# Attention in two layers: a pair's scores in three parts and its weighing in three rounds, each placed behind a round of turned blocks

## The chip, the cores and the metric

The kernel runs on one core of one Trainium2 chip, as one program. The metric is the device time of that core in microseconds, as the median of several runs. The profiled execution is one run with the hardware profiler.

The engines are named as in the profile: PE is TensorE (matmuls; PEld its weight loads), DVE is VectorE, ACT is ScalarE, POOL is GpSimd, SP the queue that issues DMAs.

## The reference, cut to what matters

The network has a first block of two layers (attention, then a mixture of experts) and a second block (gated linear attention, dilated attention, a feed-forward part). Only the attention of the first block's two layers is touched. There are 512 latent tokens and 256 context tokens, heads are 64 wide, everything is float32.

```python
def diff_attend(qb, k, v, lam):            # layer 0, four differential pairs
    s = jnp.einsum('bqhcd,bkhcd->bhcqk', qb, k).astype(jnp.float32) * ATTN_SCALE
    p = jax.nn.softmax(s, -1)
    a = p[:, :, 0] - lam * p[:, :, 1]
    return jnp.einsum('bhqk,bkhe->bqhe', a.astype(v.dtype), v)

def gqa_attend(qb, k, v):                  # layer 0, eight heads
    s = jnp.einsum('bqhgd,bkhd->bhgqk', qb, k).astype(jnp.float32) * ATTN_SCALE
    p = jax.nn.softmax(s, -1)
    return jnp.einsum('bhgqk,bkhd->bqhgd', p.astype(v.dtype), v)
```

Layer 1 has the same shape with a sink logit and a band of 128 positions (window attention) in eight heads, and a bias table over all latent keys (neighbourhood attention) in the other eight. Its queries are the 512 latents alone; layer 0 has the 256 context tokens as queries too, and these see the 256 context keys only.

## The kernel before, in words

`attention_phase` (L747 on) is called once for each layer. Its unit of work is a pair of heads for one tile of 128 queries, numbered u: eight pairs for each tile, `U` = 48 pairs in layer 0 (four latent tiles, two context tiles) and 32 in layer 1. `where(u)` gives tile n and pair p. In layer 0 the pairs p = 0 to 3 are differential (`diff` = 4): both heads' probabilities are combined into one matrix. The others, and all pairs of layer 1, keep two matrices. In layer 1 the order within a tile is: four neighbourhood pairs first, then four banded ones.

What a pair goes through:

- `score(u)` (TensorE, L943): S = q k for both heads, into `pS[u % 2]`, 1536 float32 wide, three PSUM banks. Head 0 has its operands on partitions 0-63, head 1 on 64-127. For 768 keys head 0 fills columns 0-767 and head 1 columns 768-1535, so the middle bank is shared by both (`second(u)` = 768). `pieces` cuts each head's columns at the banks; `joint` are the pieces in the shared bank, `alone` those in the outer banks. Joint pieces of head 0 come first, then the outer banks of both heads in turns, then the joint pieces of head 1. A matmul appears as two instructions in the profile. Where no more than 512 keys are seen (context queries: 256; banded pairs of the first and last tile: 512) the second head starts at column 1024 and nothing is shared. Banded pairs of the two middle tiles see 640 keys.
- `shift(u)` (VectorE): the row maximum. In layer 0 one reduction (L1145; two for 256-wide scores, L1147 and L1148) and a scaling (L1149); in layer 1 it also adds the mask or the bias and writes E (L1158, or L1163 and L1168, twice each). It waits for both `scored0` and `scored1`.
- `exp(u)` (ScalarE, L1073 or L1069): E = exp(...), two activations with row sums.
- `divide(u)` (VectorE): reciprocals (L1179); for pairs with two matrices also the scaling of head 0's (L1185). POOL scales the other head's (L929). For differential pairs `subtract(u)` (VectorE, L1192) combines both after POOL.
- `turn(u, k)` (TensorE, L974): up to four 128x128 blocks of E turned into `pT`, one bank. A round waits (`moved`) until the round before has been copied out. A pair with two matrices of 768 has 12 blocks, three rounds; of 640, rounds of 4, 4 and 2; of 512, two rounds of 4; a differential pair has 6 blocks, rounds of 4 and 2. Context pairs have one round.
- `move(u, k)`: pT to `PT[x % 4]`, four buffers. Round 0 of a pair with two matrices and more than one round is copied by VectorE (L1202), all others by ScalarE (L1084). The copy waits (`weighed`) until the buffer's contents of four rounds ago were used.
- `weigh(u, k)` (TensorE, L987 differential, L989 otherwise): probabilities times values, accumulated over the rounds in `pO`.
- `take_o(u)` (ScalarE, L1090): pO to SBUF.
- On VectorE, once for each tile of layer 0 at p = 6, four sums of squares (L1238).

The order on each engine is the order in which its code is written, with waits on semaphores between engines. TensorE's loop at L1025 is, for each u: turning round 0 of u; all scores of u+3; turning round 1; all weighing of u-1; turning round 2. ScalarE's is: copy 0 of u, exp of u+2, copy 1, take_o of u-1, copy 2. VectorE's is: `subtract(u + 1)`, copy 0 of u, then `shift(u + 3)` and `divide(u + 2)` (the other way round if pair u+2 is differential). Before it writes `pS[u % 2]`, `score(u)` waits until pair u-2 has been read: in layer 0 by exp (`e_ready`), in layer 1 by shift (`shifted`).

POOL also prepares eight rows of 1024 (L913 to L919) in layer 0 from pair 16 on, one at every second pair (four in layer 1). SP issues loads at the stage's start and waits for the last weighing before it issues the first expert weights. After the loop the output projection, the layer norm and the routing logits follow in the same stage.

Of the kernel before, what the change touches and what calls it, by code (L numbers as in the profile page):

```python
# [746 lines left out]
def attention_phase(nc, g, l, srcs, qT, kT, V, logits, na_bias):  # L747
# [11 lines left out]
    def where(u):  # L759

        return u // 8, (u + 4) % 8 if last_l else u % 8
# [18 lines left out]
    def pieces(u, b):  # L780

        out = []
        for i, k in enumerate(key_blocks(u)):
            at = b * second(u) + i * P
            if out and out[-1][0] // 512 == at // 512 and out[-1][1] + out[-1][2] == k * P:
                out[-1][2] += P
            else:
                out.append([at, k * P, P])
        return out

    def turns(u):

        n, p = where(u)
        return [(i, 0) for i in range(len(key_blocks(u)))] if p < diff else [(i, b) for i in range(len(key_blocks(u))) for b in range(2)]

    def rounds(u):
        return (len(turns(u)) + 3) // 4
# [7 lines left out]
    def k_chunk(p):  # L805
        if l == 0:
            return p if p < 4 else 4 + (p - 4) // 2
        return p // 2 if p < 4 else 2 + p - 4
# [7 lines left out]
    with Phase(nc) as ph:  # L816
# [29 lines left out]
        shared, scored0, scored1, shifted, e_ready, divided, readyD, readyP = (  # L846
            ph.sem(n) for n in ("shared", "scored0", "scored1", "shifted", "e_ready", "divided", "readyD", "readyP"))
# [10 lines left out]
        def tile(t):  # L858
            return slice(t * P, (t + 1) * P)
# [69 lines left out]
                pool.tensor_scalar(e, e, st[:, u % 4, 6 + b:7 + b], None, ALU.mult).then_inc(readyP, 1)  # L929
        @block.tensor  # L930
        def _(pe):
            def score(u):

                if u >= U:
                    return
                n, p = where(u)
                if u >= 2:
                    pe.wait_ge(shifted if last_l else e_ready, u - 1)

                def product(b, piece):  # L940
                    at, k0, w = piece
                    rows = slice(b * HD, (b + 1) * HD)
                    return pe.matmul(pS[u % 2][:, at:at + w], qT[rows, p, tile(n)], kT[rows, k_chunk(p), k0:k0 + w], start=True, stop=True)  # L943

                first, then = pieces(u, 0), pieces(u, 1)
                joint = [x for x in first if x[0] // 512 == 1], [x for x in then if x[0] // 512 == 1]
                alone = [x for x in first if x[0] // 512 == 0], [x for x in then if x[0] // 512 == 2]
                for x in joint[0]:
                    last = product(0, x)
                if joint[0]:  # L950
                    last.then_inc(shared, 1)
                for i in range(max(len(alone[0]), len(alone[1]))):
                    if i < len(alone[0]):
                        last0 = product(0, alone[0][i])
                    if i < len(alone[1]):
                        last1 = product(1, alone[1][i])
                last0.then_inc(scored0, 1)
                if joint[1]:
                    pe.wait_ge(shared, sum(second(v) == 768 for v in range(u + 1)))
                    for x in joint[1]:  # L960
                        last1 = product(1, x)
                last1.then_inc(scored1, 1)

            def turn(u, k):
                if k >= rounds(u):
                    return
                x = round_no(u, k)
                if k == 0:
                    pe.wait_ge(readyD, u + 1)
                    pe.wait_ge(readyP, u + 1)  # L970
                if x:
                    pe.wait_ge(moved, x)
                for j, (i, b) in enumerate(turns(u)[4 * k:4 * k + 4]):
                    last = pe.transpose(pT[:, tile(j)], E[:, u % NB, b, tile(i)], ident[:])  # L974
                last.then_inc(turned, 1)

            def weigh(u, k):
                if k >= rounds(u):
                    return
                (n, p), x, blocks = where(u), round_no(u, k), key_blocks(u)  # L980
                pe.wait_ge(moved, x + 1)
                if k == 0 and u:
                    pe.wait_ge(o_out, u)
                for j, (i, b) in enumerate(turns(u)[4 * k:4 * k + 4]):
                    c0, first, end = v_at(p, b), i == 0, i == len(blocks) - 1
                    if p < diff:
                        last = pe.matmul(pO[:, 0:P], PT[:, x % 4, j], V[:, blocks[i], c0:c0 + P], start=first, stop=end)  # L987
                    else:
                        last = pe.matmul(pO[b * HD:(b + 1) * HD, 0:P], V[:, blocks[i], c0:c0 + HD], PT[:, x % 4, j], start=first, stop=end)  # L989
                last.then_inc(weighed, 1)  # L990

            def turn_o(n):
                if n >= total:
                    return
                pe.wait_ge(o_ready, n + 1)
                if n:
                    pe.wait_ge(d_moved, n)
                for c in range(4):
                    last = pe.transpose(pT[:, tile(c)], o[:, n, tile(c)], ident[:])
                last.then_inc(d_turned, 1)  # L1000

            def mix(n, half, ks):
                for k in ks:
                    last = pe.matmul(pS[n % 2][:, half * 512:(half + 1) * 512], oT[:, k, tile(n)], wout[:, k, half * 512:(half + 1) * 512],  # L1004
                                     start=(k == 4), stop=(k == 3))
                return last

            def turn_f(n):
                pe.wait_ge(f_ready, n + 1)
                if n:  # L1010
                    pe.wait_ge(f_moved, 2 * n)
                for half in range(2):
                    for c in range(4):
                        last = pe.transpose(pS[half][:, 1024 + c * P:1024 + (c + 1) * P], f[:, half * 4 + c::C], ident[:])
                    last.then_inc(f_turned, 1)

            def route(n):
                pe.wait_ge(f_moved, 2 * n + 2)
                for k in range(C):
                    last = pe.matmul(pO[:, 36 * n:36 * n + 36], fT[:, k, :], wr[:, k, :], start=(k == 0), stop=(k == C - 1))  # L1020
                last.then_inc(routed, 1)

            for u in range(3):
                score(u)
            for u in range(U):  # L1025
                turn(u, 0)
                score(u + 3)
                turn(u, 1)
                if u:
                    for k in range(3):  # L1030
                        weigh(u - 1, k)
                turn(u, 2)
            for k in range(3):
                weigh(U - 1, k)
            pe.wait_ge(const_in, 16 * n_const)
            pe.wait_ge(o_out, U)
            pe.wait_ge(moved, round_no(U, 0))
            pe.wait_ge(shifted if last_l else e_ready, U)
            for n in range(total):
                if n >= 2:  # L1040
                    pe.wait_ge(x_used, n - 1)
                for half in range(2):
                    mix(n, half, range(4, 8))
                if diff:
                    if n == 0:
                        turn_o(0)
                    pe.wait_ge(d_moved, n + 1)
                    turn_o(n + 1)
                mix(n, 0, range(4))
                if n:  # L1050
                    turn_f(n - 1)
                mix(n, 1, range(4)).then_inc(mixed, 1)
                if n:
                    route(n - 1)
            turn_f(total - 1)
            route(total - 1)

        @block.scalar
        def _(act):
# [17 lines left out]
            def move(u, k):  # L1077
                if k >= rounds(u) or moved_by_vector(u, k):
                    return
                x, w = round_no(u, k), P * len(turns(u)[4 * k:4 * k + 4])  # L1080
                act.wait_ge(turned, x + 1)
                if x >= 4:
                    act.wait_ge(weighed, x - 3)
                act.activation(PT[:, x % 4].rearrange("p j n -> p (j n)")[:, 0:w], pT[:, 0:w], ACT.Copy).then_inc(moved, 1)  # L1084
# [13 lines left out]
            for u in range(U):  # L1098
                move(u, 0)
                exp(u + 2)  # L1100
                move(u, 1)
                if u:
                    take_o(u - 1)
                move(u, 2)
            take_o(U - 1)
            if diff:
                act.wait_ge(ss_ready, total)
# [1892 lines left out]
```

## Time and profile before

| what | us |
|---|---|
| median of 3 runs | 3447.9 (3446.75 to 3449.11) |
| profiled execution | 3446.33 |
| its span | 3444.5 |
| granted TensorE clock, mean | 0.942 |
| PE busy in the span | 2907.5 (84%) |
| pair loop of layer 0 in the span | about 282 to 482 |
| pair loop of layer 1 in the span | about 1330 to 1500 |

An instruction's row gives its start, its time, the engine and the line; neighbouring instructions of one kind are merged with their count. The end of a matmul is modelled, so the time that a block of matmuls takes is best read from its start to the start of the next block on the same engine. In brackets stands the idle time of the engine before the instruction and who released it.

### The profile page before, as it was taken

To read this page: it belongs to the slowest core of one execution; us is meant where nothing else is said; L and a number is where in the kernel's file an instruction comes from. 1 tells how busy PE (TensorE), PEld (TensorE's weight loads), DVE (VectorE), ACT (ScalarE), POOL (GpSimd) and SP (SyncE) were. 2 spreads that over 40 slices of the span, in tenths; PEclk is the share of its full clock that TensorE was granted. 3 is DMA by queue.
4 is the path that set the end of the run, shared out by engine and by line. 5 is a ranking of instruction groups with operands and counts; after the bars stand their busy time and mean duration, and the time that the engine had idled before them with its cause. 6 is when DMAs were issued, how large, how long until landed. Compare 5 with 4: busy or idle time off the path is not lost. (4 is left out here: it accounts for less than half of the span.)

```text
span 3444.5 us, 50705 instructions
## 1 busy us (share of the span) xinstructions
PE 2907.5 (84%) x20913; PEld 1623.6 (47%) x20913; DVE 1047.9 (30%) x2201; ACT 756.7 (22%) x1483; POOL 512.3 (15%) x632
## 2 busy tenths in 40 slices
PE   7998888678776698895866663999999999999999
PEld 4555654355444345653543332444444554544444
DVE  3425856311111444754111113443211231211101
ACT  2224641111111323620111112311112220200000
POOL 0003630233323002511322220000000000000000
PEclk8999999799999899997988886999999999999999
DMA  7833022999997642026899996112222122322237
GB/s 296 312 135 115 1 92 93 398 426 426 426 425 304 220 113 96 1 110 256 367 423 423 424 423 239 58 50 82 73 73 73 49 74 83 82 86 80 98 119 259
DMA packets 188525, 679.10 MB, mean 197 GB/s; under 512 B 52766, under 2 KB 94222, under 8 KB 163782
## 3 DMA queue, kind: packets, MB, share of 16 engines
q1 hardware_dynamic: 176550, 655.66, 49.0%
q0 software_dynamic: 11808, 21.03, 1.6%
q8 instruction: 127, 2.08, 0.2%
q14 instruction: 40, 0.33, 0.0%
HBM read 653.89 MB, written 33.98 MB: 200 GB/s over the span
## 5 line engine op out<-in xcount | busy, mean ns | idle before, releaser
L1677 PE MATMUL pH<-w,room 128*32 128x256 f32 x5504 | 340.0, 401 | 77.5 <-DMA w<-in_moe_w 77.5
L2744 PE MATMUL banks<-hT,wf 128*128 128x512 f32 (+2 forms) x768 | 303.2, 557 | 3.3 <-ACT hT L2801 2.9
L1677 PEld LDWEIGHTS pH<-w,room 128*32 128x32 f32 x5504 | 217.7, 116 | 184.7 <-issue 110.9
L1713 DVE TENSOR_TENSOR hh<-hs,pH 128x128 f32<-128x128 f32 x118 | 33.9, 287 | 794.0 <-ACT hs L1696 794.0
L929 POOL TENSOR_SCALAR E<-E,st 128x768 f32<-128x768 f32 (+3 forms) x80 | 168.0, 2100 | 661.3 <-DVE st L1179 660.7
L1684 PE MATMUL pY<-w,hT 128*32 128x256 f32 x2752 | 166.3, 381 | 107.9 <-DVE hT L1715 103.5
L2744 PEld LDWEIGHTS banks<-hT,wf 128*128 128x128 f32 x768 | 140.8, 190 | 164.6 <-issue 154.9
L416 PE MATMUL pa<-aT,w 128*128 128x512 f32 x416 | 205.7, 599 | 1.3 <-DVE aT L680 1.3
L1677 PE MATMUL pH<-room 128*32 128x256 f32 x2048 | 136.1, 424 | 57.7 <-DMA room<-in_moe_w 34.8
L1684 PEld LDWEIGHTS pY<-w,hT 128*32 128x32 f32 x2752 | 96.4, 109 | 177.8 <-issue 134.3
L2490 PE MATMUL pa<-hT,ring 128*128 128x512 f32 x384 | 167.8, 592 | 0.0
L2395 PE MATMUL pa<-hT,ring 128*128 128x512 f32 x384 | 165.0, 592 | 1.3 <-PEq L91 1.3
L974 PE MATMUL pT<-ident,E 128*128 128x128 f32 x672 | 114.6, 290 | 54.8 <-ACT PT L1084 31.2
L2783 PE MATMUL banks<-ring,aT 128*128 128x512 f32 x352 | 151.2, 592 | 0.0
L2042 PE MATMUL pa<-hT,ring 128*128 128x512 f32 x320 | 142.8, 603 | 0.0
L1004 PE MATMUL pS<-wout,oT 128*128 128x512 f32 x320 | 141.4, 594 | 0.8 <-issue 0.8
L1699 ACT ACTIVATE y<-pY 128x256 f32<-128x256 f32 x118 | 45.2, 383 | 418.2 <-PE pY L1684 418.2
L1640 POOL DMA_INDIRECT y<-y,at_y x122 | 125.9, 1032 | 60.9 <-POOL at_y L1660 59.7
L1677 PEld LDWEIGHTS pH<-room 128*32 128x32 f32 x2048 | 82.0, 122 | 106.7 <-issue 58.4
L974 PEld LDWEIGHTS pT<-ident,E 128*128 128x128 f32 x672 | 72.6, 144 | 100.3 <-issue 47.9
L1696 ACT ACTIVATE hs<-pH 128x128 f32<-128x128 f32 x118 | 32.7, 277 | 390.6 <-PE pH L1677 390.6
L943 PE MATMUL pS<-room 64*128 64x256 f32 (+2 forms) x608 | 110.7, 482 | 8.4 <-ACT E L1073 4.9
(483 smaller groups left out, 3957.8 us busy)
## 6 DMA issues: line engine op xcount, KB each, us to landing
w<-in_moe_w SPq DMA_DIRECT2D x144, 2048.0 KB
room<-in_moe_w SPq DMA_DIRECT2D x48, 2048.0 KB
mw<-in_mod_w SPq DMA_DIRECT2D x24, 2048.0 KB, 16.6
ring<-in_w_ff_down SPq DMA_DIRECT2D x33, 1024.0 KB, 4.8
ring<-in_w_in SPq DMA_DIRECT2D x15, 2048.0 KB, 8.2
ring<-in_w_gate SPq DMA_DIRECT2D x6, 2048.0 KB, 8.7
wf<-in_w_ff_gate SPq DMA_DIRECT2D x11, 1024.0 KB, 5.6
wf<-in_w_ff_up SPq DMA_DIRECT2D x11, 1024.0 KB, 8.0
```

The lines of the kernel that those rows point to most:

```text
L416: last = pe.matmul(pa[n % 2][:, 0:512], w[:, i % SLOTS_W, k, tile(c)], aT[:, k, 0:512], start=(k == 0), stop=(k == C - 1))
L929: pool.tensor_scalar(e, e, st[:, u % 4, 6 + b:7 + b], None, ALU.mult).then_inc(readyP, 1)
L974: last = pe.transpose(pT[:, tile(j)], E[:, u % NB, b, tile(i)], ident[:])
L1004: last = pe.matmul(pS[n % 2][:, half * 512:(half + 1) * 512], oT[:, k, tile(n)], wout[:, k, half * 512:(half + 1) * 512], start=(k == 4), ...
L1640: pool.indirect_dma_start(out=y_rows, out_offset=bass.IndirectOffsetOnAxis(ap=at_y[:, b:b + 1], axis=0), in_=y[:, b], in_offset=None, boun ...
L1677: last = pe.matmul(pH[strip(s), 0:2 * P].rearrange("p (j n) -> p j n", j=2), xT[:, k, :], slot_of(g, "w13", b)[:, :, k, s * P:(s + 1) * P] ...
L1684: last = pe.matmul(pY[strip(s), 0:YW], hT[:, k, :], slot_of(g, "w2", b)[:, k, s * YW:(s + 1) * YW], start=(k == 0), stop=(k == HC - 1))
L2042: last = pe.matmul(pa[b][:], ring[:, j % RING, i, tile(c)], hT[:, i, :], start=(i == 0), stop=(i == C - 1))
L2395: last = pe.matmul(pa[b][:], ring[:, j % RING, i, at], hT[:, i, :], start=(i == 0), stop=(i == C - 1))
L2490: last = pe.matmul(pa[b][:], ring[:, j % RING, k, (c % 4) * P:(c % 4 + 1) * P], hT[:, k, :], start=(k == 0), stop=(k == C - 1))
L2744: last = pe.matmul(banks[f % 2][:, j * 512 + cols.start:j * 512 + cols.stop], wf[:, i % 2, j, k, (f % 2) * P:(f % 2 + 1) * P], hT[:, k, co ...
L2783: last = pe.matmul(banks[b][:, h * 512:(h + 1) * 512], aT[:, f, tile(t)], wd[:, m % SLOTS_D, f % 2, h * 512:(h + 1) * 512], start=(f == 0) ...
```

## The change

`score(u)` gets a second argument. Part 0 is head 0's joint pieces (and the wait for the PSUM buffer), part 1 the outer banks of both heads, part 2 head 1's joint pieces. A pair without a shared bank has its whole score in part 1. For each u TensorE's order becomes: turning 0, weighing 0 of u-1, part 1 of u+3, turning 1, weighing 1 of u-1, part 2 of u+3, turning 2, weighing 2 of u-1, part 0 of u+4. On ScalarE `take_o(u - 1)` moves behind copy 2. The first three pairs' scores are still issued in one piece each.

```diff
--- before.py
+++ after.py
@@ -929,12 +929,12 @@
                 pool.tensor_scalar(e, e, st[:, u % 4, 6 + b:7 + b], None, ALU.mult).then_inc(readyP, 1)
         @block.tensor
         def _(pe):
-            def score(u):
+            def score(u, part):
 
                 if u >= U:
                     return
                 n, p = where(u)
-                if u >= 2:
+                if u >= 2 and part == 0:
                     pe.wait_ge(shifted if last_l else e_ready, u - 1)
 
                 def product(b, piece):
@@ -945,21 +945,24 @@
                 first, then = pieces(u, 0), pieces(u, 1)
                 joint = [x for x in first if x[0] // 512 == 1], [x for x in then if x[0] // 512 == 1]
                 alone = [x for x in first if x[0] // 512 == 0], [x for x in then if x[0] // 512 == 2]
-                for x in joint[0]:
-                    last = product(0, x)
-                if joint[0]:
+                if part == 0 and joint[0]:
+                    for x in joint[0]:
+                        last = product(0, x)
                     last.then_inc(shared, 1)
-                for i in range(max(len(alone[0]), len(alone[1]))):
-                    if i < len(alone[0]):
-                        last0 = product(0, alone[0][i])
-                    if i < len(alone[1]):
-                        last1 = product(1, alone[1][i])
-                last0.then_inc(scored0, 1)
-                if joint[1]:
+                if part == 1:
+                    for i in range(max(len(alone[0]), len(alone[1]))):
+                        if i < len(alone[0]):
+                            last0 = product(0, alone[0][i])
+                        if i < len(alone[1]):
+                            last1 = product(1, alone[1][i])
+                    last0.then_inc(scored0, 1)
+                    if not joint[1]:
+                        last1.then_inc(scored1, 1)
+                if part == 2 and joint[1]:
                     pe.wait_ge(shared, sum(second(v) == 768 for v in range(u + 1)))
                     for x in joint[1]:
                         last1 = product(1, x)
-                last1.then_inc(scored1, 1)
+                    last1.then_inc(scored1, 1)
 
             def turn(u, k):
                 if k >= rounds(u):
@@ -975,7 +978,7 @@
                 last.then_inc(turned, 1)
 
             def weigh(u, k):
-                if k >= rounds(u):
+                if u < 0 or k >= rounds(u):
                     return
                 (n, p), x, blocks = where(u), round_no(u, k), key_blocks(u)
                 pe.wait_ge(moved, x + 1)
@@ -1021,15 +1024,20 @@
                 last.then_inc(routed, 1)
 
             for u in range(3):
-                score(u)
+                for part in range(3):
+                    score(u, part)
             for u in range(U):
                 turn(u, 0)
-                score(u + 3)
+                weigh(u - 1, 0)
+                if u == 0:
+                    score(3, 0)
+                score(u + 3, 1)
                 turn(u, 1)
-                if u:
-                    for k in range(3):
-                        weigh(u - 1, k)
+                weigh(u - 1, 1)
+                score(u + 3, 2)
                 turn(u, 2)
+                weigh(u - 1, 2)
+                score(u + 4, 0)
             for k in range(3):
                 weigh(U - 1, k)
             pe.wait_ge(const_in, 16 * n_const)
@@ -1099,9 +1107,9 @@
                 move(u, 0)
                 exp(u + 2)
                 move(u, 1)
+                move(u, 2)
                 if u:
                     take_o(u - 1)
-                move(u, 2)
             take_o(U - 1)
             if diff:
                 act.wait_ge(ss_ready, total)
```

## Rows read from the trace of the kernel before

**Rows 1.** Table of stretches: busy time of each engine, granted clock, DMA.
```profile
core 0: us, PE busy (x) PEld busy (x) DVE busy (x) ACT busy (x) POOL busy (x), PEclk, DMA share, GB/s
296.10:413.00 116.90, 102.26 (x817) 79.20 (x816) 89.79 (x145) 74.39 (x167) 72.10 (x30) 0.99 0.15 49
413.00:450.70 37.70, 31.67 (x269) 24.18 (x268) 27.41 (x52) 23.24 (x56) 21.93 (x11) 1.00 0.00 1
450.70:479.50 28.80, 24.30 (x188) 15.35 (x188) 19.81 (x79) 21.89 (x83) 13.11 (x13) 1.00 0.01 2
1342.00:1370.70 28.70, 24.90 (x210) 18.93 (x209) 15.65 (x52) 13.81 (x34) 11.40 (x6) 0.79 0.54 175
1370.70:1387.50 16.80, 15.62 (x133) 11.38 (x132) 14.61 (x48) 11.79 (x26) 9.40 (x5) 1.00 0.00 0
1387.50:1470.70 83.20, 71.64 (x691) 53.22 (x690) 56.37 (x176) 49.56 (x113) 48.68 (x21) 1.00 0.01 1
1470.70:1500.50 29.80, 24.23 (x242) 16.71 (x242) 14.63 (x45) 15.20 (x39) 11.54 (x6) 1.00 0.01 2
```

**Rows 2.** Timeline of one G period on PE: start, us, engine, line, count, idle before.
```profile
360.26 0.63 PE L974 MATMUL pT<-ident,E 128*128 128x128 f32 x4 [0.78 <-ACT PT L1084]
360.82 1.57 PE L943 MATMUL pS<-room 64*128 64x256 f32 x8
362.32 0.66 PE L974 MATMUL pT<-ident,E 128*128 128x128 f32 x4
...
362.91 1.53 PE L989 MATMUL pO<-PT,room 128*64 128x128 f32 x24
364.37 0.66 PE L974 MATMUL pT<-ident,E 128*128 128x128 f32 x4
...
365.80 0.63 PE L974 MATMUL pT<-ident,E 128*128 128x128 f32 x4 [0.78 <-ACT PT L1084]
```

**Rows 3.** Timeline of differential pairs on PE and PEld.
```profile
337.99 1.57 PE L943 MATMUL pS<-room 64*128 64x256 f32 x8
...
341.36 0.42 PEld L974 LDWEIGHTS pT<-ident,E 128*128 128x128 f32 x4 [0.28 <-issue]
...
341.95 1.57 PE L943 MATMUL pS<-room 64*128 64x256 f32 x8
...
346.37 1.57 PE L943 MATMUL pS<-room 64*128 64x256 f32 x8
```

**Rows 4.** Groups by shape of the PE matmuls that start in 360.8 to 361.1.
```profile
L943 PE MATMUL pS<-room 64*128 64x512 f32 x1 | 0.7, 693 | 0.0
L943 PE MATMUL pS<-room 64*128 64x256 f32 x1 | 0.5, 480 | 0.0
```

**Rows 5.** Timeline: short score blocks and one weighing round, each with its follower.
```profile
459.07 0.70 PE L943 MATMUL pS<-room 64*128 64x256 f32 x4
...
459.70 0.38 PE L987 MATMUL pO<-room,PT 128*128 128x128 f32 x1
...
463.41 0.66 PE L989 MATMUL pO<-PT,room 128*64 128x128 f32 x8
464.00 0.66 PE L974 MATMUL pT<-ident,E 128*128 128x128 f32 x4
...
1475.78 1.13 PE L943 MATMUL pS<-room 64*128 64x512 f32 x4
1476.84 0.66 PE L974 MATMUL pT<-ident,E 128*128 128x128 f32 x4
```

**Rows 6.** Groups by shape, 296 to 480 us: busy, mean ns, idle.
```profile
L1073 ACT ACTIVATE E<-pS,st 128x256 f32<-128x256 f32 x32 | 14.9, 475 | 3.7 <-DVE st L1149 3.7
...
L1238 DVE CUSTOM_DVE_ANT_0 f<-o 128x128 f32<-128x128 f32 x20 | 5.9, 350 | 0.0
```

**Rows 7.** Timeline: a reduction of layer 0; layer 1 from shift to released turning.
```profile
362.81 1.76 DVE L1145 TENSOR_REDUCE st<-pS 128x2 f32<-128x1536 f32 x1
...
1372.44 0.69 DVE L1163 CUSTOM_DVE_ANT_0 E<-pS,na_bias 128x512 f32<-128x512 f32 x1 [0.95 <-PE pS L943]
...
1376.13 0.66 PE L974 MATMUL pT<-ident,E 128*128 128x128 f32 x4 [0.17 <-DVE PT L1202]
```

## Prediction

> **What bounds the kernel now.** I read first the table of stretches, to see what share of the span the change can reach, then one period of the pair loop on TensorE's own timeline, then the same period on VectorE. The change touches only the two attention stages' loops over pairs: in layer 0 the stretches 296.1 to 479.5 us, in layer 1 those from 1342.0 to 1500.5 us, 342 us of 3444.5 [rows 1]. The reader is to see there that TensorE is busy 85 to 93% of each stretch and VectorE 50 to 87%. Everything around them keeps its length and moves with them, since the stages follow one another, so what the loops gain or lose is what the kernel gains or loses.
>
> A period of a pair with two heads in layer 0 (call it G) runs from one turning to the next, 360.26 to 365.80 us: 5.54 us [rows 2]. In it TensorE turns (0.56), scores (1.50), turns (0.59), weighs all three rounds (1.46), turns (0.65) and then is idle 0.78, released by ScalarE's copy of pT. There is one pT bank, so every round of turning waits for the copy of the round before; the first two waits are covered by scoring and weighing, the last by nothing. That 0.78 us is what the change can win. A differential pair (D) has two rounds and no such hole beyond 0.2 to 0.3: its scores start 3.96 us apart at 337.99 and 341.95 [rows 3]. The next gap, 4.43 us, is the chain shift, exp, divide, shift.
>
> **What the score block costs when it is cut.** Head 0 sits on rows 0-63 and head 1 on rows 64-127 of the array. In the whole block of 1.50 us a 256-wide product (only head 0's joint piece comes so early) and a 512-wide one start within the same 0.3 us [rows 4]: head 0's joint piece runs beside head 1's lone bank, head 1's joint piece beside head 0's. Each row half has 768 columns of work, and both halves are full. After the change a joint piece stands between two blocks that use all rows, so its half of the array works alone. The nearest rows of such blocks: 256 columns beside 256 take 459.07 to 459.70, 0.63 us; 512 beside 512 take 1475.78 to 1476.84, 1.06 us [rows 5]. The slope, 0.43 us for 256 more columns in both halves, says that a half alone is no quicker than both. So the three parts cost 0.63 + 1.06 + 0.63 = 2.32 for 1.50: 0.82 us more a pair. For the 640-wide banded pairs it is, by the same slope, 0.42 + 1.06 + 0.63 = 2.11 for 1.28, the same 0.8. Bounds, as no lone half stands in this trace: below nothing more than 1.50 (if a half could share the array with its neighbours), above 2.32 plus 0.1 at each of three edges, because weighing followed by scoring is an order not seen before. I take 2.32, from the rows nearest in kind.
> The Trainium skill, page "TensorE: Matmul & The Clock Gate", Part 3, says that matmuls are "strict FIFO, no reordering", start and end in program order. By it head 0's joint piece would have had the array to itself already before, the whole block would be 0.43 + 0.85 + 0.43 + 0.2 = 1.9 us, and the cut would cost 0.4. The measured 1.50 and the two early starts speak against it here.
>
> **Weighing in three rounds.** One round of 8 takes 463.41 to 464.00, 0.59 us [rows 5]; three are 1.77 for 1.46, so two more edges of 0.15. A D pair has one more edge, 0.15.
>
> **Period by period.** TensorE's sum after is, for G, 3 x 0.59 turning + 3 x 0.59 weighing + 2.32 = 5.86 us against 5.54 now. All three copy waits are covered: between turnings stand 1.65, 1.22 and 1.22 us of other work, and a copy with its two handoffs is 0.8. The won hole (0.78) is smaller than the price (0.82 + 0.30). For D it is 3.96 - 0.28 + 0.82 + 0.15 = 4.7. Mixed ones: 4.9 (D after G) and 5.6 (G after D). Eight pairs: 4.9 + 3 x 4.7 + 5.6 + 3 x 5.86 = 42.2.
> VectorE and the second wait: once per eight pairs VectorE's four squared sums (0.35 us each [rows 6]) stand, with the subtraction, ahead of its copy of turning round 0. Now nobody waits long, since the scores are issued before round 1. After, part 2 of the scores is behind round 1; I take 1.2 us. So eight pairs cost 43.4.
> Layer 0: three eights, 130.2 + 0.8 (first parts at the half clock) for 116.9 [rows 1]: +14.1. The 37.7 us after them: 24.7 for five pairs, 14.7 for the three whose next scores are 256 wide (a shorter score block, but only 0.59 between later turnings, 0.2 of wait each): 39.4, +1.7. The context pairs: PE's wait for E now comes at the end of a period, before the next turning, and an exp stands on ScalarE behind the copy: 0.66 + 0.60 + two exps of 0.47 [rows 6] with a handoff is 2.3 where G pairs now need 1.8 to 2.0; D pairs stay on their exp chain of 2.4. +2 together. Layer 0: +17.8.
>
> **The new circle in layer 1.** VectorE runs in order: copy round 0 of u, shift u+3, divide u+2, copy round 0 of u+1. Shift u+3 needs all scores of u+3. Now those are issued before turning round 1. After, part 2 stands behind round 1, which waits for VectorE's copy. This makes a ring: scores end, shift, reciprocal and scaling, copy, turning 1, weighing 1, part 2. From shift to the released turning: 1372.44 to 1376.13, 3.69 us [rows 7], with a 512-wide row scaled; most are wider. From there 0.59 + 0.59 + 0.63, and 0.24 from the next block's start until the shift (1372.20 to 1372.44, 1370.70 and 1.50 before it): 2.05. In all 5.74, taken as 5.8 us, per pair whose coming scores are 768 wide, however little TensorE has to do. In layer 0 the shift is one reduction of 1.76 us [rows 7] for four operations that fill some 2.3; the ring is 5.2 to 5.5, below the sum of 5.86, and D pairs' copy is ScalarE's.
> Stretch 1370.7 to 1387.5: four pairs, now 3.7 to 5.3 us with VectorE back to back, after 4 x 5.8 = 23.2 for 16.8: +6.4. The 83.2 us after are twice eight pairs: 3 x 5.63 (640-wide scores; sum 1.77 + 1.77 + 2.11) + 5.5 + 4 x 5.8 = 45.6 for 41.6: +8.0. First stretch: half-clock scores +1.1, the rest +0.8. Last stretch (512-wide scores, not cut): -0.1 to -0.2 a pair, and the last three, with weighing under the copies, -0.4 each: -1.0 in all with what the ring still adds. Layer 1: +15.3.
> Sum: +33.1 us on the profiled execution's 3446.3 (span 3444.5 and 1.8 around it), 3479.4. That execution lies 1.6 below the median 3447.9, so 3481.
>
> ScalarE's take_o one place later costs nothing: it has the period's last weighing, part 0 and the next turning as cover, 1.8 us for 0.3; without that cover it would delay weighing round 0 by 0.3. The moves of SP and POOL: none is touched; POOL's 2.6 us a pair has 5.8 now.
>
> **Rivals.**
> 1. Ring absent or hidden: VectorE's copy comes soon enough in layer 1, TensorE's sum alone decides. Then the four pairs cost 4.7 to 5.0 and the eights 45.6 - 1.9: -4.3 - 3.8, 3473. For it: VectorE's busy share is only 68% in the 83.2 us stretch; against it: the order in its queue.
> 2. The cut costs edges alone, 0.4 a score: 29 cut scores of layer 0 give back 12 us, the ring 2: 3467. By the FIFO rule of the Trainium skill's page named above, this is what would come. Against it: rows 4 and 5.
> 3. The other side, faster: a lone half overlaps its full-row neighbours, so scores stay 1.5. G is then 5.0 for 5.54, layer 0 falls by some 7, layer 1's ring of 5.4 still adds 3: 3444. It decides from 0.7 us of overlap for each cut score. Against it: all turnings and weighings use 128 rows, and the block after a score starts only when its stream has ended.
> 4. More than forecast: every new edge costs 0.1 more (four a pair, some 220 in all, half of them under waits: 11 us), and the half clock lasts longer at layer 1's start: +8 to +14, about 3491.
>
> **How the numbers follow.** Forecast 0.62, rival 1 0.13, rival 2 0.06, rival 3 0.04, rival 4 0.15. The terms' own bounds put the forecast at 3473 to 3489; 8 in 10 need rival 1 below and most of rival 4 above: 3466 to 3495. Within 0.2% (7 us, about what can be told from no change) is part of rivals 2 and 3, 0.03; faster 0.03; slower 0.94.
>
> **What would show it.** In the profile after: TensorE's timeline with a 256-wide x2 block of 0.6 us between two turnings or weighings, no idle before turning round 0 in layer 0, a G period of 5.8 to 5.9 and D of 4.7; in layer 1 periods of 5.8, and idle before turning round 1, released by VectorE's copy. Wrong would be: a lone joint piece of 0.4 us or less until the next block, G periods under 5.5, or layer 1 pairs at 4.7 with VectorE's copy waiting for TensorE.

## The result, and the profile after

The changed kernel takes 3493.2 us (3483.3 to 3495.1) where before, in the same comparison, takes 3447.3: ratio 1.013, 95% interval 1.0112 to 1.0149. It is 46 us slower; the forecast was 33 (3481, range 3466 to 3495).

The profiled execution of the changed kernel is its quickest: span 3481.4 us for 3444.5, +36.9. Measured from the first turning to the start of what follows the last weighing, the pair loop of layer 0 went from 188.9 to 210.9 us and that of layer 1 from 159.4 to 172.3. That is 34.9 of the 36.9. The rest is a start of the first loop 2.1 us earlier, 1 us less between the loops, and 5.0 us more behind the second one; those come from a jump of 6.4 us at about 2297 us of before's span (2327 of the changed kernel's), in a stage that is the same in both kernels; see "Behind the loops" below.

Periods worked out from the starts of the turnings, eight pairs together (us):

| pairs | before | after | forecast of after |
|---|---|---|---|
| layer 0, 0-7 | 38.5 | 44.3 | 43.4 + 0.8 |
| 8-15 | 38.5 | 43.6 | 43.4 |
| 16-23 | 40.5 | 47.0 | 43.4 |
| 24-31 | 37.9 | 40.1 | 39.4 |
| 32-47 (context) | 33.7 | 35.9 | +2 |
| layer 1, 0-7 | 40.6 | 41.6 | |
| 8-15 | 41.5 | 49.4 | 45.6 |
| 16-23 | 41.6 | 45.7 | 45.6 |
| 24-31 | 35.7 | 35.5 | -1 |

(The forecast's stretches for layer 1 are cut by scores, three pairs apart from these; the rows fit roughly.)

First the table of stretches of the changed kernel, columns as in [rows 1], cut at its own turnings: layer 0 in three pieces, then layer 1 from its start on.
```profile
293.00:428.00 135.00, 125.97 (x819) 76.41 (x819) 82.40 (x143) 75.08 (x167) 72.14 (x31) 0.96 0.14 46
428.00:468.00 40.00, 35.46 (x267) 22.72 (x266) 26.33 (x54) 22.96 (x56) 22.32 (x11) 1.00 0.00 1
...
1359.80:1385.90 26.10, 24.20 (x211) 16.61 (x211) 16.11 (x55) 14.87 (x34) 11.79 (x6) 0.94 0.64 209
1385.90:1407.20 21.30, 16.28 (x127) 9.04 (x126) 11.78 (x38) 10.22 (x23) 8.79 (x4) 1.00 0.00 1
1407.20:1420.00 12.80, 12.74 (x83) 8.47 (x84) 6.90 (x22) 6.01 (x14) 4.91 (x2) 0.73 0.00 1
```
TensorE's busy share in layer 0 rose from 87% [rows 1] to 93% while the same 817 to 819 matmuls took longer, and its idle time fell from 14.6 to 9.0 us. So the longer time is in blocks that take longer (lone halves, more edges between blocks, and a lower clock, 0.96 for 0.99), not in waits. In layer 1 it is the other way in 1385.9 to 1407.2: 76% busy where [rows 1] had 93% for the same kind of pairs; and right behind it the granted clock is 0.73.

TensorE's timeline of one G period of layer 0, the answer to [rows 2]:
```profile
326.26 1.13 PE L943 MATMUL pS<-room 64*128 64x512 f32 x4
327.32 0.66 PE L977 MATMUL pT<-ident,E 128*128 128x128 f32 x4
327.90 0.66 PE L992 MATMUL pO<-PT,room 128*64 128x128 f32 x8
328.49 0.70 PE L943 MATMUL pS<-room 64*128 64x256 f32 x2
329.12 0.66 PE L977 MATMUL pT<-ident,E 128*128 128x128 f32 x4
329.70 0.66 PE L992 MATMUL pO<-PT,room 128*64 128x128 f32 x8
330.29 0.70 PE L943 MATMUL pS<-room 64*128 64x256 f32 x2
330.92 0.66 PE L977 MATMUL pT<-ident,E 128*128 128x128 f32 x4
331.50 0.66 PE L992 MATMUL pO<-PT,room 128*64 128x128 f32 x8
```
No row has an idle time. A lone joint piece (x2, 256 wide) takes 328.49 to 329.12, 0.63 us, as long as two halves side by side in [rows 5]; the outer banks 1.06, a weighing round 0.59. The period is 5.81 to 5.83 us (forecast 5.86, before 5.54).

Layer 1, from one shift to the turning it releases, the answer to [rows 7] (1395.59 is turning 0 of the next pair; one x1 at 1399.61 is the first matmul of its turning 1):
```profile
1393.78 0.66 PE L977 MATMUL pT<-ident,E 128*128 128x128 f32 x4 [1.58 <-DVE PT L1210]
...
1394.37 0.66 PE L992 MATMUL pO<-PT,room 128*64 128x128 f32 x8
...
1394.96 0.70 PE L943 MATMUL pS<-room 64*128 64x256 f32 x4
...
1395.59 0.66 PE L977 MATMUL pT<-ident,E 128*128 128x128 f32 x4
1395.79 0.69 DVE L1171 CUSTOM_DVE_ANT_0 E<-pS,na_bias 128x512 f32<-128x512 f32 x1 [2.06 <-issue]
...
1396.77 1.13 PE L943 MATMUL pS<-room 64*128 64x512 f32 x4
...
1398.87 0.68 DVE L1210 COPY PT<-pT 128x512 f32<-128x512 f32 x1
...
1399.61 0.33 PE L977 MATMUL pT<-ident,E 128*128 128x128 f32 x1 [1.71 <-DVE PT L1210]
```
This is the ring, whole: turning 1 at 1393.78, weighing 1, part 2 (in the x4 block at 1394.96, with part 0 of the next score), shift at 1395.79, VectorE's copy at 1398.87, the next turning 1 at 1399.61. 5.83 us, and TensorE waits 1.71 of them for the copy.

### The profile page after: what moved, and what is told of

Its sections match the earlier page's. It is cut to its first block and busy times, and to the rows that moved or that the text cites. A ratio compares the mean times of both kernels' runs of the same rounds, so it can differ in the third digit from the quotient of the medians.

```text
span 3481.4 us, 50729 instructions
## 1 busy us (share of the span) xinstructions
PE 2952.4 (85%) x20913; PEld 1616.3 (46%) x20913; DVE 1036.7 (30%) x2201; ACT 759.1 (22%) x1483; POOL 512.1 (15%) x632
## 5 line engine op out<-in xcount | busy, mean ns | idle before, releaser
L1685 PEld LDWEIGHTS pH<-w,room 128*32 128x32 f32 x5504 | 217.7, 115 | 184.4 <-issue 107.5
L943 PE MATMUL pS<-room 64*128 64x256 f32 (+2 forms) x608 | 150.4, 499 | 11.2 <-ACT E L1081 7.7
L977 PE MATMUL pT<-ident,E 128*128 128x128 f32 x672 | 115.9, 292 | 38.5 <-DVE PT L1210 15.9
```

The costliest lines, as they stand in the source:

```text
L1685: last = pe.matmul(pH[strip(s), 0:2 * P].rearrange("p (j n) -> p j n", j=2), xT[:, k, :], slot_of(g, "w13", b)[:, :, k, s * P:(s + 1) * P] ...
```

## The experiments

Loop times below are the two loops' (before 188.9 and 159.4, changed 210.9 and 172.3). Ratios are against before, with 95% intervals. Several of the kernels need not be faster; they take one part of the change each.

**e1_same**: no edit.

> The changed kernel once more, nothing edited. The first profile gave pair loops of 210.9 us (layer 0) and 172.3 us (layer 1) where before had 188.9 and 159.4; its other three executions were 9 to 12 us slower than the profiled one. Theory (lost overlap of the two array halves, ring through VectorE's copy in layer 1, and half-clock stretches that TensorE's holes in the ring bring on): block times repeat to 0.01 us (0.63, 1.06, 0.59), ring periods 5.7 to 5.9 repeat, and what varies between executions is the number of half-clock stretches in and behind the two loops, 3 to 7 us each. Rival (the spread is DMA or expert stage): the loops repeat within 1 us and the spread lies in the expert stages. Time 3483 to 3495.

Measured: 3492.6 us (3484.1 to 3497.5), 1.0126 (1.0111 to 1.0142). This profile has span 3495.6, 14.2 more than the first one of the same program. Loops 218.4 and 174.7, and 3.5 more behind them. The block times repeat; what differs is the clock. The same stretch of both profiles, columns as above. This one's:
```profile
421.00:461.00 40.00, 34.84 (x191) 20.89 (x190) 21.68 (x37) 18.44 (x42) 20.40 (x10) 0.83 0.00 1
```
The first one's:
```profile
421.00:461.00 40.00, 34.24 (x245) 21.43 (x246) 26.61 (x48) 22.33 (x53) 26.21 (x12) 1.00 0.00 1
```
The mean clock of 0.83 is some 13 us at 1.2 GHz, the rest at 2.4. The two counts of matmuls (191 and 245) don't compare the clock alone, since the windows do not hold the same pairs; the same pairs do: 23 and 24 take 10.30 and 6.96 us here, 7.67 and 5.03 in the first profile. So the scatter of the changed kernel is, for these two profiles, mostly half-clock stretches in the loops. The rival, the expert stages, fails for the loops' 9.9 us; 3.5 us do lie behind them.

**e2_score3**: scores in three parts, weighing in one piece.
```diff
                 turn(u, 0)
-                weigh(u - 1, 0)
 ...
                 turn(u, 1)
-                weigh(u - 1, 1)
+                for k in range(3):
+                    weigh(u - 1, k)
                 score(u + 3, 2)
                 turn(u, 2)
-                weigh(u - 1, 2)
```

> Only the scores are cut in three (part 1 behind turning 0, part 2 behind the whole weighing, part 0 behind turning 2); weighing stays in one piece behind turning 1. Theory: the ring now has the whole weighing in it, so it gets longer: layer 0 G pairs 3.4 + 0.59 + 1.46 + 0.63 + 0.24 = 6.3 us (5.83 in the changed kernel), layer 1 6.2 to 6.6 (5.4 to 5.9): some 5 us more in layer 0 and 10 more in layer 1, about 3500. Rival (TensorE's sum alone decides, no ring): two edges less, G 5.5 to 5.7, and a time of about 3470 to 3475.

Measured: 3508.2 us, 1.0183 (1.017 to 1.0197); loops 216.7 and 184.4. Layer 0 G pairs 6.19, layer 1 from pair 6 to 24 5.7 to 6.9 (pairs 7 and 8 7.7, in and behind a half-clock stretch). The time is 8 us over the expected 3500. TensorE has two edges less to do and is slower; a ring with the weighing in it explains that, and the waits show it: 6.26 us is the changed kernel's 5.83 and the 0.44 by which the whole weighing (1.03) is longer than one round (0.59), to 0.01. TensorE's timeline, two turnings 1 of layer 1 one ring of 6.26 us apart, each with its wait:
```profile
1400.53 0.66 PE L977 MATMUL pT<-ident,E 128*128 128x128 f32 x4 [2.17 <-DVE PT L1209]
1401.11 1.09 PE L992 MATMUL pO<-PT,room 128*64 128x128 f32 x16
1402.14 0.70 PE L943 MATMUL pS<-room 64*128 64x256 f32 x4
...
1406.79 1.11 PE L977 MATMUL pT<-ident,E 128*128 128x128 f32 x4 [2.30 <-DVE PT L1209]
```

**e3_weigh3**: weighing in three rounds, scores whole.
```diff
                 weigh(u - 1, 0)
-                if u == 0:
-                    score(3, 0)
-                score(u + 3, 1)
+                for part in range(3):
+                    score(u + 3, part)
                 turn(u, 1)
                 weigh(u - 1, 1)
-                score(u + 3, 2)
                 turn(u, 2)
                 weigh(u - 1, 2)
-                score(u + 4, 0)
```

> Only the weighing is cut in three rounds, one behind each turning; the scores are whole again (the three parts issued one straight after the other behind weighing round 0), take_o behind copy 2 as in the changed kernel. Theory: score block back to 1.50 us, no ring, G pairs 3 x 0.59 + 3 x 0.59 + 1.50 + two waits of 0.2 = 5.4 us (5.54 before), D pairs 3.9 to 4.0; layer 0 loop 186 to 189, layer 1 155 to 160, time 3440 to 3448. Rival (the cut weighing is what cost the time): G pairs 5.8, time above 3465.

Measured: 3447.0 us, 1.0002 (0.9993 to 1.0011): as before. Loops 193.9 and 154.0; layer 0 misses the expectation by 5 us. A G period of layer 0 takes 5.42 us as expected. TensorE's timeline has the score block back at 1.49 (326.45 to 327.94) and a wait of 0.19:
```profile
325.30 0.63 PE L977 MATMUL pT<-ident,E 128*128 128x128 f32 x4 [0.19 <-ACT PT L1089]
325.86 0.66 PE L992 MATMUL pO<-PT,room 128*64 128x128 f32 x8
326.45 1.57 PE L943 MATMUL pS<-room 64*128 64x256 f32 x8
327.94 0.66 PE L977 MATMUL pT<-ident,E 128*128 128x128 f32 x4
```
Layer 0 loses it again in pairs that I had priced unchanged: the G pair after a D pair takes 5.73 (before 5.24), the context pairs 35.3 for 33.7, and pair 1, which falls in a half-clock stretch, 5.74 for 3.68. Of layer 1's gain of 5.4 us, 3.8 are its first two pairs, which ran mostly at full clock here and at half clock in before's profile. So the loss of the change comes with cutting the scores and placing the parts apart, the moved wait for exp included; the weighing's cut alone is neutral in time.

**e4_part2_early**: part 2 directly behind part 1.
```diff
                 score(u + 3, 1)
+                score(u + 3, 2)
                 turn(u, 1)
                 weigh(u - 1, 1)
-                score(u + 3, 2)
```

> Head 1's joint piece is issued straight behind the outer banks (part 2 behind part 1, before turning 1), all else as in the changed kernel. Theory: parts 1 and 2 in a row overlap again (head 1's half goes on while head 0's is done): 1.5 us for both instead of 1.06 + 0.63; the ring through VectorE's copy is gone, so layer 1 periods fall from 5.7-5.9 to 4.5-5.3, its loop from 172 to 159-163; layer 0 G 5.8 to 5.9 (0.2 of wait is now open between turnings 1 and 2), D pairs 4.4 to 4.6 (parts 2 and 0 no longer side by side); time 3468 to 3476. Rival (no ring, layer 1's loss is TensorE's sum): layer 1 loop changes by less than 3 us.

Measured: 3464.8 us, 1.0056 (1.0042 to 1.0069); loops 197.7 and 160.1. Moving one matmul of 0.63 us by two blocks gives back 28 of 46 us. Layer 1's pairs 5 to 7 take 4.46 for 4.04, 5.69 and 5.82, pairs 8 to 23 5.37 to 5.44. In layer 0 G pairs are 5.8 as expected, and the pairs at the tile's end, which I had left as they were, fall from 6.4 and 7.7 to 5.8 and 5.9: that is 4.2 us. This kernel also has no half-clock stretch at 397 or 1407 us. Its loops are only 9.5 us longer than before's; of the 18.5 us of its profiled span over before's the rest lies outside them.

**e5_halves**: built on before. Scores whole behind turning 0, the weighing cut in the middle of round 1, a fifth buffer for turned blocks, and (not in the cut below) `take_o(u - 1)` behind copy 2 as in the changed kernel.
```diff
+        def pt(x):
+            return PT[:, x % 5] if x % 5 < 4 else fT[:, 0:4]
 ...
                 turn(u, 1)
-                if u:
-                    for k in range(3):
-                        weigh(u - 1, k)
+                split = u and rounds(u) == 3 and rounds(u - 1) == 3
+                weigh(u - 1, 0)
+                weigh(u - 1, 1, range(2) if split else range(4))
+                if not split:
+                    weigh(u - 1, 2)
                 turn(u, 2)
+                if split:
+                    weigh(u - 1, 1, range(2, 4))
+                    weigh(u - 1, 2)
```

> Built on the kernel before: scores stay whole behind turning 0. Where pairs u and u-1 both have three rounds the weighing is cut in the middle of round 1: six blocks behind turning 1, the rest behind turning 2. A fifth buffer for turned blocks (fT, idle in the loop) lets ScalarE's copy of round 1 start before weighing round 0; take_o behind copy 2. Theory: the score block stays at 1.50, one more edge of 0.15, and each half of the weighing (0.66 + 0.15 = 0.81) just covers a copy with its handoffs (0.78): layer 0 G pairs 3 x 0.59 + 1.50 + 1.62 = 4.9 us for 5.54, D pairs as before; layer 1 pairs 4.9 to 5.0 (scores 640 wide: 4.7) for 5.34 and 4.4 to 4.7 for 5.06. Layer 0 loop 178 to 182 us, layer 1 loop 148 to 152, time 3428 to 3434. Rival (a wait elsewhere, VectorE or POOL, sets the pace once the copy is covered): G pairs stay at 5.3 or more and the time within 3440 to 3448.

Measured: 3432.6 us, 0.9955 (0.9942 to 0.9968), against 3447.1. G pairs 4.88 (5.54 before), layer 1 from pair 9 to 27 4.4 to 4.9. Loops 186.8 and 142.3: layer 1 6 us better than expected, layer 0 5 to 9 worse, since pairs 15 and 23 take 8.25 and 8.37 (before 6.20 and 6.19). Which share of the gain the new cut, the buffer and `take_o` have was not taken apart.

**e6_act_copy**: the changed kernel, ScalarE copies turning round 0 in layer 1.
```diff
-            return r == 0 and where(u)[1] >= diff and rounds(u) > 1
+            return not last_l and r == 0 and where(u)[1] >= diff and rounds(u) > 1
```

> The changed kernel with one edit: in layer 1 ScalarE, not VectorE, copies turning round 0. Theory (the ring of layer 1 closes through VectorE's queue): with VectorE's copy out of the ring, layer 1's periods fall to TensorE's sum or to ScalarE's order (copy 0 now stands ahead of exp u+2): 4.5 to 4.9 for pairs 5 to 7, 5.3 to 5.7 for the others; layer 1 loop 163 to 167 for 172 to 175, and fewer half-clock stretches behind it. Layer 0 unchanged (211 to 218). Time 3474 to 3484. Rival (it is TensorE's sum, not the ring): periods stay at 5.7 to 5.9 and the loop at 172 to 175.

Measured: 3481.2 us, 1.0111 (1.0096 to 1.0127); loops 212.4 and 167.4. The ring pairs of layer 1 fall with nothing changed for TensorE: pairs 6 and 7 from 5.69 and 5.82 to 5.25 and 4.33, pairs 14 to 17 from 5.76-5.98 to 5.40-5.60. Its first two pairs are in a half-clock stretch (+3.7 us against the changed kernel), which the changed kernel has at pairs 8 and 9 instead (+3.7); so the ring itself is worth some 5 us, the loop's 4.9. Pairs 10 to 13 take 5.40 to 5.62 with and without the ring: there TensorE's own sum decides.

**e7_halves_sq5** and **e8_after_sq5**: VectorE's sums of squares one pair earlier, in the kernel with halves and in the changed one.
```diff
-                if diff and p == 6:
+                if diff and p == 5:
```

> The kernel with the weighing in halves, with one edit: VectorE's four sums of squares of a tile of layer 0 stand one pair earlier (p = 5 for p = 6), between two pairs with two matrices and no longer ahead of the subtraction of the next tile's first pair. Theory: the periods of pairs 15 and 23 (8.3 and 8.4 us, other G pairs 4.9) have VectorE's queue in them, squares and subtraction ahead of its copy of turning 0; without the squares there they fall to 5.0 to 5.5, and with the hole the half-clock stretches behind it (368, 409 us) go: layer 0 loop 180 to 182 for 186.8, time 3424 to 3428. Rival (the subtraction behind POOL's row sets it): they stay above 6.5 and the time at 3430 to 3434.

> The same edit in the changed kernel. Theory: its periods of pairs 7, 15 and 23 (6.4, 7.7 and 7.7 to 10.3 us, TensorE's sum 5.83) fall to 5.9 to 6.3, 4 to 6 us in all, with fewer half-clock stretches in layer 0: loop 204 to 208 for 211 to 218, time 3483 to 3488. Rival (the hole at the tile's end has another owner): loop within 1 us of 211 where the clock is the same.

Measured: e7 3429.6 us, 0.9954 (0.994 to 0.9967), loops 185.5 and 142.2; pairs 15 and 23 8.37 and 6.82. e8 3488.1 us, 1.013 (1.0111 to 1.0148), loops 212.9 and 172.2; pairs 14 and 15 6.78 and 6.83, together no less than the 5.83 and 7.67 before the edit. So the squares are not the owner and my theory fell: pair 15 of e7 does not move, and pair 23 gives only 1.55 of 3.5 us. The timeline of e5_halves within its long pair 15 names another:
```profile
360.17 2.78 POOL L916 TENSOR_SCALAR mrow<-mrow 128x1024 f32<-128x1024 f32 x1
...
363.05 2.21 POOL L932 TENSOR_SCALAR E<-E,st 128x768 f32<-128x768 f32 x1
...
365.29 1.02 DVE L1202 SCALAR_TENSOR_TENSOR E<-E,st 128x768 f32<-128x768 f32 x1 [0.56 <-POOL E L932]
366.23 0.68 DVE L1212 COPY PT<-pT 128x512 f32<-128x512 f32 x1
...
366.96 0.66 PE L977 MATMUL pT<-ident,E 128*128 128x128 f32 x4 [1.90 <-DVE PT L1212]
```
POOL's row of 1024 stands ahead of its scaling for the next differential pair, VectorE's subtraction waits for that scaling, and the copy that TensorE needs stands behind the subtraction.

**e9_halves_swap** (on e5_halves) and **e10_after_swap** (on the changed kernel): the copy ahead of the subtraction.
```diff
-                subtract(u + 1)
                 move(u, 0)
+                subtract(u + 1)
```

> The kernel with the weighing in halves (squares at p = 6, as before), with one edit in VectorE's loop: its copy of turning round 0 of u stands ahead of the subtraction of u+1. Moving the squares did not shorten the long periods at a tile's end; in the trace the subtraction of pair 8 or 16 waits for POOL's scaling (which stands behind one of POOL's rows of 1024 or starts late) with the copy behind it. Theory: with the copy first the periods of pairs 15 and 23 (8.3 us) fall to 4.9 to 5.6 and the half-clock stretches behind them go: layer 0 loop 178 to 181 for 186.8, time 3422 to 3427. Rival (the next turning waits for the same subtraction anyway, so the hole only moves by one pair): pair 15 falls but pair 16 rises by the same, time 3429 to 3433.

> The same swap in the changed kernel: copy of turning 0 of u ahead of the subtraction of u+1. Theory: pairs 7, 15 and 23 (6.4, 7.7, 7.7 to 10.3 us) fall to TensorE's sum, 5.8 to 6.0: 4.3 us less in layer 0 and fewer half-clock stretches; loop 204 to 207, time 3480 to 3487; layer 1, where nothing is subtracted, keeps its 172 to 175. Rival: the hole moves to the next pair, loop 211 to 218.

Measured: e9 3424.3 us, 0.9933 (0.9919 to 0.9946), pairs 15 and 23 5.29 and 5.28; only pairs 17 and 25 pay for it, 4.53 for 4.06. No half-clock stretch in layer 0 after 300 us; loops 181.7 and 146.0 (layer 1's first two pairs are mostly at half clock, 3.8 us more than in e5). e10 3486.9 us, 1.0118 (1.0103 to 1.0134), pairs 7, 15 and 23 5.84, 6.10 and 6.10, but pair 18 7.15 for 6.49; loops 208.6 (expected 204 to 207) and 172.2. The timeline of e9 at the same place: the copy no longer waits, TensorE waits 0.34.
```profile
363.84 0.68 DVE L1212 COPY PT<-pT 128x512 f32<-128x512 f32 x1
...
364.47 1.02 DVE L1202 SCALAR_TENSOR_TENSOR E<-E,st 128x768 f32<-128x768 f32 x1
364.58 0.66 PE L977 MATMUL pT<-ident,E 128*128 128x128 f32 x4 [0.34 <-DVE PT L1212]
```
e9 is the fastest kernel of the study, 23 us below before.

## Why the prediction was right, and where it missed

**Two readings first.** The prediction read TensorE as busy 85 to 93% of each stretch; [rows 1] give 81% (the last stretch) to 93%. And it took all three eights of latent pairs as equal, though before's third has 40.5 us for 38.5.

**The cut score block.** Right to the hundredth: 0.63 + 1.06 + 0.63. The overlap of the two row halves was the price, and in e3, with the parts side by side again, the block is back at 1.49. The Trainium skill ("TensorE: Matmul & The Clock Gate", Part 3) states that matmuls start and end strictly in program order, which would have made the cut cost 0.4. That does not hold here: it would have left G pairs near 5.4 to 5.5, measured 5.83.

**The cut weighing.** 0.59 a round, right. Weighing before scoring, an order not seen before, costs nothing more (327.90 to 328.49).

**D pairs, forecast 4.7.** Wrong in the sum: a pair with two rounds has nothing between part 2 of u+3 and part 0 of u+4, so the two lone halves stand side by side and overlap. TensorE's timeline shows four instructions of both parts in one block: in pair 9 without a wait, in pair 10 with one of 0.5 for exp in it. The last row is turning 1 of pair 12, the G pair behind the D pairs:
```profile
345.69 0.70 PE L943 MATMUL pS<-room 64*128 64x256 f32 x4
346.33 0.66 PE L977 MATMUL pT<-ident,E 128*128 128x128 f32 x4
...
349.14 0.61 PE L990 MATMUL pO<-room,PT 128*128 128x128 f32 x4
349.68 1.46 PE L943 MATMUL pS<-room 64*128 64x256 f32 x4
...
358.56 0.66 PE L977 MATMUL pT<-ident,E 128*128 128x128 f32 x4 [0.64 <-DVE PT L1210]
```
Without a wait it is 0.64 for both parts, and TensorE's sum is 3.99 (pair 9). Pairs 10 and 11 took 4.75 and 4.26, 0.8 and 0.3 more, for the chain shift, exp, divide. Pair 8, 5.03 (forecast 4.9), has no wait: behind a G pair a weighing round stands between the two parts. Pair 12, forecast 5.6, took 6.32, since its turning 1 waits for VectorE's copy, a wait that the prediction had at nothing. So D pairs 9 to 11 are 1.1 us under the forecast, pairs 8 and 12 0.8 over it and the tile's end 0.6 over it. That the eight came out at 43.6 for 43.4 is these misses cancelling, and luck.

**The moved wait for exp.** I had priced it for the context pairs only (+2, measured +2.2; but e3, in which the wait for exp stays ahead of the whole score, has 1.6 more there too, so this +2 was met partly by luck). In layer 0 it also stands ahead of the turning behind a D pair: part 0 waits for exp of u+2. The timeline of all engines around pair 18 of the changed kernel:
```profile
391.50 2.35 POOL L917 TENSOR_TENSOR mrow<-mrow,r 128x1024 f32<-128x1024 f32 x1
391.96 1.91 DVE L1157 TENSOR_SCALAR st<-st 128x2 f32<-128x2 f32 x1
...
393.91 0.90 ACT L1081 ACTIVATE E<-pS,st 128x768 f32<-128x768 f32 x1 [2.65 <-DVE st L1157]
...
395.84 0.70 PE L943 MATMUL pS<-room 64*128 64x256 f32 x2 [1.81 <-ACT E L1081]
```
Pair 18 takes 6.49 us (before 5.26), 1.74 more than pair 10 at the same place, and VectorE's scaling ahead of that exp takes 1.91 for 0.17, 1.74 more, beside POOL's row. That is half of what the third eight has over the forecast (47.0 for 43.4); another 1.35 is pair 19 (5.61 for 4.26), in the half clock that follows. e4 keeps this wait but has part 2 earlier, and its pairs 10 and 18 both take 4.41: there exp comes in time, and VectorE's scaling is done before POOL's row starts to hold it. No experiment undid the wait alone, so its share is read from these rows, not shown.

**The tile's end.** Size right (1.2 forecast; 0.6, 1.8 and 1.8 measured), owner wrong: VectorE's copy stands behind the subtraction, which waits for POOL; the squares are a small part (e7 to e10).

**The ring in layer 1.** Forecast 5.8, measured 5.69 to 5.98 where it binds, 5.83 in the rows above; the 640-wide pairs 5.6, forecast 5.63. It sets in one pair later than forecast: pair 5 takes 4.04. The four pairs from 5 on still sum to the forecast 23.2, because pair 8 has 1.75 us of half clock in it: luck. Three edits moved it as a ring should move: longer by the weighing put into it (e2), gone with part 2 outside it (e4), gone with another engine's copy (e6). Rival 1 is out.

**The size of the whole.** The sum of +33.1 for the profiled execution met +36.9, but by misses of both signs: layer 0 +22.0 (forecast +17.8), layer 1 +12.9 (forecast +15.3; its first five pairs are 3.1 us shorter than before's, mostly because they ran at full clock, where the forecast had +1.9), and +2.0 outside the loops, forecast nothing. The median is 12 us above the forecast: 3.8 are this difference, and the profile shows the kernel's quickest execution, 9.9 below its median, where before's lies 1.6 below.

The step that failed is the clock term: "0.8 (first parts at the half clock)" in layer 0 and 1.1 in layer 1 were the only half-clock costs in the sum. The changed loops bring on new ones. In layer 1 the granted clock is at 1.2 GHz from 1407.3 us on for 6.8 us, right behind three ring pairs in which TensorE idled 1.6 to 1.7 us each; there pairs 8 and 9 take 7.65 and 7.92, where pairs 16 and 17, of the same kinds, take 5.90 and 5.98. Such a stretch of 3 to 7 us at 1407 to 1412 is in all five profiles with the whole ring (changed, e1, e2, e8, e10) and in none of the seven without it (before, e3, e4, e5, e6, e7, e9; a half clock of 3 to 14 us at the loop's start is in all). In layer 0 the hole at pair 18 is followed by one at 397 to 399 us in every profile with the changed layer 0 loop (changed, e1, e6, e8, e10), and e1 has 10 us more at 425.

Rival 4 named about 3491, and the median is there by number, not by its mechanism. Of its two terms the first, 11 us for dearer edges, did not come (blocks cost what was forecast), and the second, a longer half clock at layer 1's start, did not either (3.4 us in the changed kernel's profile, 13.7 in e1 and in before). That the new stretches make the 9.9 us between profile and median is shown for the pair of profiles (14.2 us apart, 9.9 in the loops), not for each execution.

**Behind the loops.** The prediction had everything around the loops keep its length. It does not: the 5.0 us come from a jump of 6.4 us in one place, where nothing is changed (1.4 us are won back elsewhere). The row of before, then that of the changed kernel:
```profile
2296.29 14.00 PE L2042 MATMUL pa<-hT,ring 128*128 128x512 f32 x32
```
```profile
2330.66 5.80 PE L2050 MATMUL pa<-hT,ring 128*128 128x512 f32 x7 [3.59 <-issue]
```
TensorE stands idle 3.59 us after one instruction of this block, with no wait that the profile shows, and 6.8 us at the half clock begin at 2328.9. The seven profiles in which parts of the scores stand apart (changed, e1, e2, e4, e6, e8, e10) all have this idle time, 3.5 to 3.9 us at the same place; before, e3, e5, e7 and e9 have none there (e5, e7 and e9 idle 4.2 to 4.5 us some 34 us later, where before idles 1.8). So it goes with the program and is no scatter, and some 5 of the 46 us are not made in the loops. What causes it stays open.

## What to carry to other kernels

Matmuls on different row halves of the array fill each other's time only while they stand next to each other; before moving a half-array matmul to fill a gap, compare the gap (here 0.78 us) with what its partner loses (0.82). Before putting work behind a wait, follow its result through the queues of the other engines: if it comes back to that wait, it is a ring, and where it is longer than the busiest engine's own sum, its length is the period. The gap was there to be filled by work that costs one edge: the weighing cut into two equal halves, with a buffer more so that the copy need not wait, gave 0.9955, and an order on VectorE that nothing needed cost another 8 us. And a sum that meets the measured total may do so by misses that cancel: compare it term by term, and the stages outside the change too.

## What the runs showed of the hardware

- A lone 256-wide float32 product on 64 rows holds TensorE for 0.63 us until the next block; two of them, one on each row half, take the same (0.63 in [rows 5], 0.64 from 345.69 to 346.33). In the whole score block a 512-wide product starts within 0.3 us of the 256-wide one that is issued ahead of it [rows 4]; that it is the other head's is inferred.
- VectorE's 128x2 operation (L1157, 0.17 us elsewhere) took 1.91 us beside POOL's two-input operation on 128x1024 (391.50 to 393.85), and both end together. A reduction keeps its 1.76 us beside POOL's rows.
- The same program's profiles differ by 14.2 us in 3490; 9.9 of it lie in the two loops, where block times at full clock repeat and the half-clock stretches differ.
